# Hybrid decoder step: a level's products ahead of the sampled sequences' first threshold count on TensorE

## The reference: what is computed

```
h1 = LN1(alpha*x  + 0.5*SwiGLU_1(x))
h2 = LN2(alpha*h1 + W_out[attention heads | recurrent heads])
y  = LN3(alpha*h2 + 0.5*SwiGLU_2(h2))
```

```
f = lb + (1 - lb) * sigmoid(W_f x)
S_t = diag(f_t) S_{t-1} + (1 - f_t) i_t^T
o_t = S_t^T q_t
```

## Time and profile before

| what | value |
|---|---|
| median of 3 runs | 2456.15 us |
| profiled execution: its own time | 2458.99 us |
| profiled execution: span of the trace | 2457.3 us |
| TensorE (PE) busy | 2371.4 us, 97% |
| VectorE (DVE) busy | 1670.3 us, 68% |
| ScalarE (ACT) busy | 700.9 us, 29% |
| GpSimd (POOL) busy | 862.8 us, 35% |
| mean granted TensorE clock | 0.984 of full |

### The profile page before, as it was taken

The page is one execution under the profiler, slowest core; times in us unless marked ns, Lnnn a source line. Parts: engine busy times, 40 slices in busy tenths (PEclk is TensorE's granted clock), DMA queues, the critical chain, the costliest instruction groups (busy, mean ns, idle before and its releaser), DMA issues.

```text
span 2457.3 us, 33403 instructions
## 1 busy us (share of the span) xinstructions
PE 2371.4 (97%) x12317; PEld 1943.0 (79%) x12317; DVE 1670.3 (68%) x2677; ACT 700.9 (29%) x1406; POOL 862.8 (35%) x924
## 2 busy tenths in 40 slices
PE   8999999999999999999999899999999999999996
PEld 7888888888887636777777777788878888888885
DVE  5675666578984178898778856335576665677886
ACT  1122222210023156772222255513222222210014
POOL 4344444446473021110000111414244444445570
PEclk9999999999999999999999889999999999999999
DMA  6021222374211114320000111121012221157301
GB/s 181 18 95 52 86 70 88 108 258 148 104 57 35 45 47 120 103 86 18 2 18 2 48 27 46 39 67 37 10 61 86 69 84 63 61 194 267 142 18 69
DMA packets 137151, 192.31 MB, mean 78 GB/s; under 512 B 18728, under 2 KB 85368, under 8 KB 136736
## 3 DMA queue, kind: packets, MB, share of 16 engines
q1 hardware_dynamic: 129328, 169.71, 20.6%
q0 software_dynamic: 7664, 20.47, 2.9%
HBM read 160.10 MB, written 30.06 MB: 77 GB/s over the span
## 4 chain that ended last, share of the span: by engine, by line
PE 85%; DVE 9%; issue 2%; DMA 2%; ACT 1%; POOL 1%; SPq 0%; DVEq 0%; POOLq 0%; ACTq 0%
PE ps L1981 38%; PE ps L2075 14%; PE ps L727 8%; PE ps L732 6%; PE ps L1089 4%; PE ps L977 2%; PE ps L951 2%; PE ps L2078 2%; PE ps L772 1%; PE ps L867 1%; PE ps L785 1%; PE ps L964 1%; DMA down_weights<-ffn_wd 1%; PE ps L795 1%; PE ps L917 1%
## 5 line engine op out<-in xcount | busy, mean ns | idle before, releaser
L1981 PE MATMUL ps<-big 128*128 128x258 f32 x1760 | 413.7, 383 | 5.1 <-DVE big L2394 4.6
L1981 PEld LDWEIGHTS ps<-big 128*128 128x128 f32 x1760 | 335.5, 191 | 57.5 <-issue 7.0
L2246 ACT ACTIVATE down_weights<-ps 128x258 f32<-128x258 f32 x370 | 142.5, 386 | 706.5 <-PE ps L1981 706.4
L2514 DVE TENSOR_TENSOR down_weights<-ps,down_weights 128x258 f32<-128x258 f32 x330 | 139.4, 425 | 265.5 <-ACT down_weights L2246 190.5
L727 PE MATMUL ps<-acts,weight_ring 128*128 128x344 f32 x768 | 241.1, 464 | 0.0
L727 PEld LDWEIGHTS ps<-acts,weight_ring 128*128 128x128 f32 x768 | 143.5, 193 | 79.2 <-issue 15.5
L2075 PE MATMUL ps<-big,aux 128*128 128x258 f32 x840 | 192.2, 383 | 4.0 <-DVE big L2627 4.0
L2822 POOL TENSOR_TENSOR big<-weight_ring 128x256 f32<-128x256 f32 x100 | 75.1, 753 | 336.1 <-PE ps L1981 301.7
L2075 PEld LDWEIGHTS ps<-big,aux 128*128 128x128 f32 x840 | 159.9, 191 | 29.6 <-DVE big L2627 5.6
L732 PE MATMUL ps<-weight_ring,acts 128*128 128x256 f32 (+3 forms) x720 | 175.7, 398 | 0.0
L732 PEld LDWEIGHTS ps<-weight_ring,acts 128*128 128x128 f32 (+1 forms) x720 | 127.1, 181 | 33.2 <-issue 2.8
(11 more groups left out here) (447 smaller groups left out, 4520.1 us busy)
## 6 DMA issues: line engine op xcount, KB each, us to landing
big<-scratch_hidden SPq DMA_DIRECT2D x12, 2838.0 KB, 11.0
weight_ring<-ffn_wd SPq DMA_DIRECT2D x8, 2816.0 KB, 9.8
scratch_hidden<-down_weights SPq DMA_DIRECT2D x40, 516.0 KB, 2.8
weight_ring<-ffn_wg SPq DMA_DIRECT2D x20, 1024.0 KB, 7.9
weight_ring<-ffn_wu SPq DMA_DIRECT2D x20, 1024.0 KB, 8.4
down_weights<-ffn_wd SPq DMA_DIRECT2D x4, 2816.0 KB, 20.3
weight_ring<-w_in SPq DMA_DIRECT2D x9, 1024.0 KB, 5.4
big<-x_prompt SPq DMA_DIRECT2D x8, 512.0 KB, 6.1
```

Source lines behind the costliest of these rows:

```text
L1981: last = M(PS[:, 3 * e + bank, 0:TQ], lhs[:, i, :], rhs[:, i, :], start=begin and i == 0, stop=end and i == n - 1, skip_group_check=True)
L2246: A(st(e, c), PS[:, 3 * e, 0:TQ], ACT.Copy).then_inc(cp_done, 1)
L2514: V.tensor_tensor(out, PS[:, 3 * e + bank, 0:TQ], st(e, part), ALU.add).then_inc(add_done, 1)
```

## The change

In each recurrence level TensorE's list has the level's products first and then the level's first count. It was the other way round. Nothing else is edited: no instruction is added or removed, and the lists of the other four engines stay as they are.

```diff
             for t in range(4):
                 for lv in range(NPASS):
+                    level_products(t, lv)
                     if (t, lv, 0) in DEC_SLOTS:
                         count(DEC_SLOTS.index((t, lv, 0)))
-                    level_products(t, lv)
                     here = BESIDE[t][lv]
                     if len(here) > 1:
                         unit(here[0])
```

## The result

The changed kernel takes 2488.18 us (median of 4 runs, 2488.13 to 2490.91); the kernel before took 2452.85 in the 4 runs it was compared with. The ratio is 1.0152, 95% interval 1.0134 to 1.017. 2478 was predicted from the 2456.15 known then, with a range of 2467 to 2490. As a difference, 22 us were predicted (11 to 34 as a range) and 37 us (1.52% of 2456) measured: the right direction, and too small. The two medians lie 35.3 us apart. In later runs the kernel before had a median of 2450.24 (17 runs, made beside the first four experiments) and of 2451.64 (29 runs, beside the others, from 2444.59 to 2458.28).

A forecast was written before the change was run, and what follows sets the result against it. TensorE was taken to bound blocks 0 to 2, with VectorE close. Span 2457.3 + 16.7 (order) + 5.2 (clock) = 2479.2; adjusted to the runs' median, 2478 us, with an 8-in-10 range of 2467 to 2490.

The forecast's parts named there:

- What bounds the stage, and the ring: Blocks 0 to 2: TensorE bounds; its counts and VectorE's comparisons wait on each other; neighbouring second counts wait about 2.1 us.
- The products no longer hidden, and the waits given back: +16.7: Twelve levels with neighbouring counts: 15.4 + 3.2 + 0.3 us exposed, 1.9 and 0.4 given back in levels 3 and 7.
- Block 2, levels 3 and 4, hidden behind VectorE: VectorE's work covers the products there: cost 0 in level 3, about 0.3 us in level 4.
- under 7: Sign of being right: block 2 loses under 7 us.
- Level 7 and the end of a block; units between the counts; no knock-on: Level 7 of blocks 0 and 1 gives back 0.4 us; remaining units cover the turnaround; later instructions shift about equally.
- The clock: 3 falls x 1.72 = 5.2: Blocks 0 to 2: new waits drop TensorE to half clock in three levels, 1.72 us each, 5.2 us in all.
- every fourth level: Assumed rate of clock falls among the 12 levels with neighbouring counts, giving three falls.
- The upper bound of the term, 20.6: Clock term with one fall in each of the 12 levels: 12 x 1.72 = 20.6 us.
- the clock falls in most of the 12 levels: Rival for blocks 0 to 2: 16.7 + 10 x 1.72 = 33.9 us slower, 2490 us; chance 0.15.
- The sum by that section: Whole loss if small idle spells make the clock swing, as the skill's second section says: up to 37 us.

The follow-up runs named there:

- the first four experiments: Changed order with eight matmuls in each wait, with four, in level 6 alone, with a unit always between counts; ratios 1.0072, 1.0107, 1.0062, 1.0015 against the kernel before.
- eight fillers: Changed kernel plus eight matmuls of 128 columns, their results overwritten, between the two counts of each neighbouring pair: 2466.97 us, ratio 1.0072 to the kernel before.
- level 6 alone: Kernel before, with the products put ahead of the first count only in level 6 of each block: 2466.36 us, ratio 1.0062.
- products first where apart: Kernel before, with the products ahead of the first count only where a unit stays between the counts, and in level 7: 2449.02 us, ratio 0.9992.

## Why the prediction was too small, step by step

- **What bounds the stage, and the ring.** Right. TensorE's wait at a neighbouring second count is 2.10 us, as forecast. The counts are 2.48 apart and not 2.38, because the first count now stands straight behind the level's products and shows 0.39 us (1127.09 in the timeline above), where behind a unit it showed 0.28 (1127.08 in the earlier trace rows).
- **The products no longer hidden, and the waits given back: +16.7.** Right. With the clock kept up by eight fillers it measures 17.6 us (13.7 to 21.3). Block 0 alone, from level 1's products to block 1, took 64.6 us before and 71.9 with the fillers, with no fall in either: 7.3 for a forecast of 6.3. The 0.1 us per pair above is part of the difference.
- **Block 2, levels 3 and 4, hidden behind VectorE.** Right at full clock (7.85 and 4.22 us, with the fillers). In the changed kernel itself it didn't show, since slower units had made TensorE late: block 2 lost 10.2 us, where under 7 was named as a sign of being right, and its waits in levels 3 and 4 were 2.10 and 2.17 us and not longer ones. With the fillers block 2 lost 3.5.
- **Level 7 and the end of a block; units between the counts; no knock-on.** Right: with the units between them the counts cost nothing that can be told, block 3 starts 36.2 us later, and its last products (1416.56 against 1380.38) are still 36.2 us later.
- **The clock: 3 falls x 1.72 = 5.2.** This is the term that failed. The changed kernel has 12 falls at the 12 pairs, not 3. The difference to the run with eight fillers is 20 to 21 us of time and 24.0 us in the blocks, for 61.4 us more at half clock: 2.0 us per pair by the blocks. Two sizes were wrong, the number above all. The rate "every fourth level" had no row behind it. The nearest row, a wait of 2.73 us with a fall, was discounted because two waits came together there, and that was a misreading of rows 7 and 10: the clock fell at 1291.4, and the wait of 1.40 us ran from 1292.5 to 1293.9, so it came after the fall. In the window at full clock TensorE was idle for 6.90 - 4.17 = 2.73 us, the first wait alone. One wait had been enough, and in the changed kernel one of 2.10 is. As to the size, 1.72 was the price of a fall of 3.4 us behind a unit of 344 columns, but half of the new falls last 6.8 us. The upper bound of the term, 20.6, is about what came. The rival "the clock falls in most of the 12 levels" had this mechanism and 33.9 us, against 37 measured, and I gave it 0.15.
- **The Trainium skill.** The section "Loop structure matters more than you think" of the page "TensorE: Matmul & The Clock Gate" says that matmuls that follow each other, with copies by other engines beside them, keep the clock, and that a long wait before each loses it. I read it as leaving waits of 2 us alone. That reading is wrong here: waits of 2.10 us brought half clock 12 times of 12. The runs agree with its section "A second HAM failure mode: psum-queue depth-cycling", by which small idle spells between groups of matmuls are enough. The sum by that section was given as up to 37.
- **The range.** The changed kernel's median, 2488.18, is under the upper end of 2490 only because the kernel before ran faster in the comparison (2452.85) than the 2456.15 from which the range was built; as a difference, 37 us is above the 34. That upper end was set at ten falls of 1.72; the upper bound itself, with 2.0 per pair, gives 2456 + 17 + 24 = 2497. Also the page's single execution (2458.99) lay at the slow end of the runs of this kernel, so a trace-to-trace comparison with it makes the kernel before look some 7 us slower than its median.

## What to carry to other kernels

When two engines pass work back and forth, look for what fills the turnaround on the busier one, and before moving it away ask what will stand there. Price an exposed wait on TensorE twice: for its own length, and for the matmuls behind it that run at half clock; where a row shows one fall after a wait of that size, count a fall for every such wait until a run says otherwise, and check in the clock's own windows which wait came ahead of it. Useless matmuls in the wait tell the two prices apart in a single run.

## What the runs showed of the hardware

A wait of 2.10 us (once 2.17) between two matmuls of 4 columns brought a half-clock stretch of 3.4 or 6.8 us in 15 of 15 cases (12 in the changed kernel, 3 with level 6 alone). Of the 15, the seven that began before the second of the two matmuls started lasted 6.8 us and the eight that began after it 3.4. With four matmuls of 128 columns and a wait of 1.10 to 1.22 us a fall came in 3 of 11; with eight and 0.21 to 0.27 us in none of 11. In the old order the wait of 2.73 us at block 2's level 3 brought a fall in all four traces that have it (the kernel before twice, level 6 alone, products first where apart), and the wait of 0.68 us at block 1's level 3 in three of four, where its like in block 0 brought none in four. Eight matmuls of 128 columns took 2.03 us. The mean granted clock of whole executions moved with it: 0.979 in the median for the changed kernel, 0.987 for the kernel before, 0.991 with the eight fillers.
